# A chunked recurrence on four corners of TensorE, with merged products and one place in PSUM per chunk

## What is computed

```python
def step(state, inp):
    r_t, w_t, k_t, v_t, kk_t, a_t = inp
    sa = jnp.einsum('bhvk,bhk->bhv', state, -kk_t)
    state = (state * w_t[:, :, None, :] + sa[..., None] * (kk_t * a_t)[:, :, None, :]
             + v_t[..., None] * k_t[:, :, None, :])
    return state, jnp.einsum('bhvk,bhk->bhv', state, r_t)
...
mu = jnp.mean(y, -1, keepdims=True)
var = jnp.mean(jnp.square(y - mu), -1, keepdims=True)
y = ((y - mu) * lax.rsqrt(var + RWKV_GN_EPS)).reshape(B, T, C)
```

## Time and profile before

| | |
|---|---|
| median of three runs | 2672.34 us (2670.58 to 2675.16) |
| the profiled execution | 2671.66 us |
| its span, first to last instruction | 2669.8 us |
| TensorE (PE) busy over the span | 97% |
| VectorE (DVE) / ScalarE (ACT) / GpSimd (POOL) busy | 66% / 39% / 3% |
| mean granted TensorE clock | 0.990 |

### The profile page before, as it was taken

How to read it: one execution, slowest core, us unless ns; L and a number is a source line. 1 busy time by engine, 2 the same in 40 slices (tenths; PEclk the granted TensorE clock), 3 DMA queues, 4 the chain that set the end, 5 groups by cost and what they waited for, 6 DMA issues and landing times. The chain is left out here.

```text
span 2669.8 us, 46706 instructions
## 1 busy us (share of the span) xinstructions
PE 2600.5 (97%) x19152; PEld 2151.7 (81%) x19152; DVE 1765.2 (66%) x2819; ACT 1041.2 (39%) x1839; POOL 88.0 (3%) x121
## 2 busy tenths in 40 slices
PE   8999999999999999899999998999999999999998
PEld 7788888888777788888888887777778788888887
DVE  6877667678344564577777775853446867667676
ACT  4332223445433534344444444542343332223443
POOL 0000000000000000111111110000000000000000
PEclk9999999999999999899999999999999999999999
DMA  4332335454423388521111110630022332335454
GB/s 143 111 105 76 118 114 180 151 196 155 99 95 102 104 265 219 138 50 36 34 38 38 30 42 6 248 135 1 32 102 80 110 116 70 113 114 192 139 190 145
DMA packets 268722, 295.65 MB, mean 111 GB/s; under 512 B 64898, under 2 KB 199296, under 8 KB 268544
## 3 DMA queue, kind: packets, MB, share of 16 engines
q1 hardware_dynamic: 265808, 290.47, 34.2%
q10 hardware_dynamic: 2736, 2.65, 0.4%
HBM read 206.47 MB, written 81.36 MB: 108 GB/s over the span
## 5 line engine op out<-in xcount | busy, mean ns | idle before, releaser
L1141 PE MATMUL f_ps<-hi,f_wh 128*128 128x512 f32 x672 | 263.1, 391 | 4.1 <-DVE f_wl L847 4.1
L1143 PE MATMUL f_ps<-hi,f_wl 128*128 128x512 f32 x672 | 262.9, 391 | 0.0
L2543 PE MATMUL f_ps<-hi,f_ahead_h 128*128 128x512 f32 x392 | 164.0, 418 | 0.8 <-PEq L72 0.8
L2544 PE MATMUL f_ps<-one_lo,f_ahead_h 128*128 128x512 f32 x392 | 153.6, 392 | 0.0
L2545 PE MATMUL f_ps<-hi,f_ahead_l 128*128 128x512 f32 x392 | 153.6, 392 | 0.0
L1141 PE MATMUL f_ps<-f_t3h,f_t2h 128*128 128x512 f32 x392 | 152.5, 389 | 0.0
L1142 PE MATMUL f_ps<-f_t3l,f_t2h 128*128 128x512 f32 x392 | 152.5, 389 | 0.0
L1143 PE MATMUL f_ps<-f_t3h,f_t2l 128*128 128x512 f32 x392 | 152.5, 389 | 0.0
L1141 PEld LDWEIGHTS f_ps<-hi,f_wh 128*128 128x128 f32 x672 | 127.0, 189 | 31.2 <-DVE f_wl L847 4.9
L1143 PEld LDWEIGHTS f_ps<-hi,f_wl 128*128 128x128 f32 x672 | 126.7, 189 | 26.4
L1142 PE MATMUL f_ps<-one_lo,f_wh 128*128 128x512 f32 x352 | 137.6, 391 | 0.0
(11 more groups left out here) (584 smaller groups left out, 6830.4 us busy)
## 6 DMA issues: line engine op xcount, KB each, us to landing
act<-one_y SPq DMA_DIRECT2D x30, 512.0 KB, 3.5
f_work<-act SPq DMA_DIRECT2D x30, 512.0 KB, 3.6
act<-y SPq DMA_DIRECT2D x30, 512.0 KB, 3.6
arena<-act SPq DMA_DIRECT2D x30, 512.0 KB, 3.7
one_y<-in_w_in SPq DMA_DIRECT2D x25, 512.0 KB, 4.4
early<-in_ffn_w_gate SPq DMA_DIRECT2D x11, 1024.0 KB, 6.2
early<-in_ffn_w_up SPq DMA_DIRECT2D x11, 1024.0 KB, 8.7
f_raw<-in_ffn_w_gate SPq DMA_DIRECT2D x10, 1024.0 KB, 6.2
```

The source lines that it names most:

```text
L1141: nc.tensor.matmul(out, wh, xh, start=start, stop=False)
L1143: return nc.tensor.matmul(out, wl, xh, start=False, stop=stop)
L2543: nc.tensor.matmul(dense_ps[:, b, cols], w_hi[:, b, k, :], hi[:, k, cols], start=(k == 0), stop=False)
L2544: nc.tensor.matmul(dense_ps[:, b, cols], w_hi[:, b, k, :], lo[:, k, cols], start=False, stop=False)
```

## The change

**Crossed pairs.** For pairs 2 and 3 the results of most products go to the other half of the partitions: operand rows 0 to 63, result partitions 64 to 127, and the reverse. The matmuls of a group are issued in the order of pairs 0, 2, 1, 3, so that four in a row use the four different corners of the array. Two products, `tf` and `gr`, stay straight (`STRAIGHT`). The operands of pairs 2 and 3 are loaded into the rows that this needs, which alternates with the chunk (`crossed`): some loads become three (`load_pairs`), a second copy of two operands for these pairs is loaded (`load_across`, into an unused part of `hi`), and the end decays are exchanged between the halves once at the start of the stage (two DMAs and a copy on GpSimd).

**Merged products.** `gram_l` is part of `gram_b`; `turn_b` and `turn_k` are `turn_bk`; `turn_a` and `x` are `ax`; each level's `y` is `yt`, which also turns the inverse so far with the identity; then only `t` follows. `tt` and VectorE's `start` are gone; a product `tf` on the last level gives the turned factor for `wu`. There are 20 products per chunk where there were 27.

**One place in PSUM.** All products of a chunk are written to the same place, two pairs in each of the two banks, so each product waits until the last result has been taken out. Results of 16 matmuls are taken out in one wide copy.

**Mean.** `mean` multiplies with a centering matrix in two halves of 128 columns; ScalarE copies the centered values out and squares them from PSUM; VectorE's subtraction is gone.

The planner's assumed times are changed with it (`ON_PE`, `OUT_OF`), and so the order.

```diff
-PRODUCTS = ["gram_b", "gram_k", "gram_l", "turn_a", "turn_b", "turn_k", "x",
-            *[f"{w}{lv}" for lv in range(LEVELS) for w in (("y", "t", "tt") if lv + 1 < LEVELS else ("y", "tt"))],
-            "wu", "gr", "s", "out", "mean", "var"]
+PRODUCTS = ["gram_b", "gram_k", "turn_bk", "ax", *[f"{w}{lv}" for lv in range(LEVELS) for w in ("yt", "t") if (w, lv) != ("t", LEVELS - 1)],
+            "tf", "wu", "gr", "s", "out", "mean", "var"]
+STRAIGHT = {"tf", "gr"}
...
+def load_pairs(sp, dst, src, exchange, sem):
+    for r in range(2) if exchange else ():
+        sp.dma_start(dst[rows_of(r)], src[rows_of(1 - r)]).then_inc(sem, 16)
+    if not exchange:
+        sp.dma_start(dst, src).then_inc(sem, 16)
+
+def load_op(sp, c, which, ops, ops_dram, ops_in):
...
+    if crossed(c) == (which in (0, 3)):
+        load_pairs(sp, dst[:, 0:2], src[:, 0:2], False, ops_in[j])
+        load_pairs(sp, dst[:, 2:4], src[:, 2:4], True, ops_in[j])
+    else:
+        load_pairs(sp, dst, src, False, ops_in[j])
+
+def load_across(sp, c, ARx, ops_dram, ops_in):
+    for w, which in enumerate((0, 3)):
+        src = ops_dram[which].rearrange("(q p) t -> p q t", p=P)[:, 2:4, c * CH:(c + 1) * CH]
+        load_pairs(sp, ARx[c % 2][:, :, w, :], src, not crossed(c), ops_in[c % 2])
...
+            for r in range(2):
+                sp.dma_start(decay_x[rows(r)], end_decay[rows(1 - r), 2:4, :]).then_inc(decay_in, 16)
...
-                def group(k, lhsT, rhs, width=CH):
-                    for p in range(PAIRS):
-                        for h in range(2):
...
-                            mm = nc.tensor.matmul(at(k, p, h, width), lhsT[rows(h), p], moving, start=True, stop=True)
+                def at(p, r, block, width=CH):
+                    return ps[j][rows(r), p // 2, (p % 2 * 4 + block) * CH:(p % 2 * 4 + block) * CH + width]
+                corners = [(p, r, 1 - r if p >= 2 and name not in STRAIGHT else r) for p in (0, 2, 1, 3) for r in range(2)]
+                def group(*parts):
+                    for block, lhsT_of, rhs_of, width in parts:
+                        for p, r, to in corners:
+                            mm = nc.tensor.matmul(at(p, to, block, width), lhsT_of(p)[rows(r)], rhs_of(p)[rows(r)], start=True, stop=True)
...
+                def sum_of(*terms):
+                    for n in range(2):
+                        for x_, (lhsT_of, rhs_of) in enumerate(terms):
+                            for p, r, to in corners[4 * n:4 * n + 4]:
+                                mm = nc.tensor.matmul(at(p, to, 0), lhsT_of(p)[rows(r)], rhs_of(p)[rows(r)], start=(x_ == 0),
+                                                      stop=(x_ == len(terms) - 1))
...
+                    group((0, lambda p: B[j][:, p], unit, CH), (1, lambda p: K[j][:, p], unit, CH))
+                elif name == "ax":
...
+                    group((0, lambda p: AR[j][:, p, 0, :], unit, CH), (1, lambda p: GK[j][:, p, 0, :], lambda p: V[j][:, p], CH))
...
+                    group((0, lambda p: LTm[j][:, lv, p], lambda p: T0[j][:, p], CH), (1, lambda p: T0[j][:, p], unit, CH))
+                elif name == "tf":
+                    act(f"yt{LEVELS - 1}")
+                    group((0, lambda p: YT[j][:, p, 0, :], lambda p: YT[j][:, p, 1, :], CH))
+                elif name[0] == "t":
+                    act(f"yt{name[1:]}")
+                    group((0, lambda p: YT[j][:, p, 1, :], lambda p: YT[j][:, p, 0, :], CH))
...
+                    for n in range(2):
+                        mm = nc.tensor.matmul(features(j)[:, n * P:(n + 1) * P], center[:, 1 if n and not crossed(c) else 0, :],
+                                              yb[j][:, 2 * n:2 * n + 2].rearrange("p q c -> p (q c)"), start=True, stop=True)
...
-                    nc.vector.tensor_tensor(TT0[j][:], GB[j][:, :, 0, :], over_pairs(m_one[:, 1]), ALU.mult).then_inc(by_dve[j], 1)
-                    nc.vector.tensor_tensor(TT0[j][:], TT0[j][:], over_pairs(eye[:]), ALU.add).then_inc(by_dve[j], 1)
...
-                    for which in (("queries", 0), ("keys", 0), ("keys", 1), ("queries", 1), ("queries", 2)):
+                    for which in (("across", 0), ("queries", 0), ("keys", 0), ("keys", 1), ("queries", 1), ("across", 1), ("queries", 2)):
```

More of the change, by code:

```diff
@@ L1472, in joint_plan @@
[L1472 to L1483, removed]
+                      "yt0": [out_of("ax"), ("masked", c)],
+                      "s": [out_of("gr"), out_of("s", c - 1)],
+                      "var": [("square", c)]}.get(name, [n and out_of(PRODUCTS[n - 1])])
@@ L1484, in joint_plan @@
+            event(("rw", c, name), "pe", ON_PE.get(name, 0.47), *before)
+            event(("out_of", c, name), "dve" if name in TO_DVE else "act", OUT_OF.get(name, 0.58), ("rw", c, name),
+                  name == "s" and c and ("rw", c - 1, "out"))
+            if name == "gram_b":
+                event(("masked", c), "pool", 4.6, out_of(name))
             if name == "mean":
@@ L1627, in attend_and_recur @@
         pn = numbered(PRODUCTS)
-        dn = numbered(["gram_b", "gram_k", "gram_l", "one_t", "start", *[x for x in PRODUCTS if x in TO_DVE and x[0] == "t"], "gr_r", "gr", "mean"])
-        an = numbered(["turn_a", "turn_b", "turn_k", "x", *[f"y{lv}" for lv in range(LEVELS)], "wu", "out", "square", "var"])
+        dn = numbered(["gram_b", "gram_l", "gram_k", *[f"t{lv}" for lv in range(LEVELS - 1)], "tf", "gr_r", "gr"])
+        an = numbered(["turn_bk", "ax", *[f"yt{lv}" for lv in range(LEVELS)], "wu", "out", "mean", "square", "var"])
         gn = numbered(["one", "start", *[f"lev{lv}" for lv in range(LEVELS)]])
@@ L1637, in over_pairs, with result, by_bank, both @@
             return tile.unsqueeze(1).broadcast_to([P, PAIRS, CH])
[L1639 to L1643, removed]
+        def result(j, at, width=CH):
+            return ps[j][:].rearrange("p b (x c) -> p b x c", x=2)[:, :, :, at * CH:at * CH + width]
+        def by_bank(tile):
+            return tile.rearrange("p (b x) c -> p b x c", b=2)
+        def both(tile):
+            return tile.rearrange("p (b x) w c -> p b x (w c)", b=2)
+        def all_pairs(mask):
+            n = mask.shape[-1]
+            return mask.unsqueeze(1).unsqueeze(1).broadcast_to([P, 2, 2, n])
+        def features(j):
+            return ps[j][:, 0, 0:PAIRS * CH]
+        def across(c, p):
+            return AR[c % 2][:, p] if p < 2 else ARx[c % 2][:, p - 2]
         def chunk(c):
@@ L1812, in recur @@
                 elif name == "gram_k":
-                    if c >= 2:
-                        dve("mean", c - 2)
-                    group(1, K[j], AR[j], 2 * CH)
-                elif name == "gram_l":
-                    dve("gram_b")
-                    group(0, AR[j][:, :, 0, :], B[j])
-                elif name == "turn_a":
+                    dve("gram_l")
+                    group((0, lambda p: K[j][:, p], lambda p: flat(across(c, p)), 2 * CH))
+                elif name == "turn_bk":
@@ L1869, in recur @@
[L1869 to L1876 removed]
+                    if c:
+                        pe.wait_ge(state, c)
+                    else:
+                        pe.wait_ge(zeroed, 1)
@@ L2990, in recurrence_tables @@
         "mean_all": np.full((P, P), 1.0 / RW, f),
+        "center": np.stack([np.eye(P, dtype=f)[m] - (same.astype(f) / f(CH))[m] for m in (n, (n + CH) % P)], 1),
         "eye": (s == t).astype(f),
```

226 lines of the change are left out of this document (98 added, 128 removed).

## The result

The changed kernel takes 2568.83 us (median of four runs, 2567.76 to 2569.63) against 2673.47 us before, measured beside it (2670.58 to 2675.16): ratio 0.961, 95% interval 0.9599 to 0.9622. The forecast was 2572 us. Later measurements of the kernel before, beside the experiments, gave medians of 2672.21 to 2672.70 us, and one of the changed kernel 2567.76 us.

A forecast was written before the change was run, and what follows sets the result against it. TensorE, busy 97% of the span, was taken as the bound: 2671.7 - 112 (products) + 10 (idle) + 2 (loads) = 2571.7, so 2572 us, chance 0.66; own range 2552 to 2590, 8-in-10 range 2548 to 2615.

The forecast's parts named there:

- What bounds the stage: In the changed stage TensorE, busy 563 of 581 us, sets the pace, so time taken from it comes off the end.
- A round of four at the price of a round of two: Four matmuls on four corners take 0.117 us, as two did: products 17.5 to 10.5 us per chunk, 112 us in all.
- The number of products and matmuls is no gain: Per chunk on TensorE: 8 more small matmuls; 7 fewer group starts give only 0.35 of the 7.0 us saved.
- four corners never run at once: Rival: row halves writing the same partitions exclude each other, so small matmuls keep the old price; 2675 us, chance 0.06.
- VectorE and ScalarE: In the stage VectorE loses 57 us, leaving 369; ScalarE's wider copies add 17 us, hidden under TensorE.
- One place in PSUM costs nothing: Each product's wait for the last take-out costs nothing in itself; other chunk and attention fill TensorE meanwhile.
- Loads: SyncE's extra DMA issues, per chunk and before the stage: mostly covered, 2 us added, bounds 0 and 13.
- the mark that I named for it: Sign that the loads were mis-sized: the stage begins later than 1086 us.
- Added idle: TensorE idle in the stage grows by 10 us, as fewer long recurrence groups cover attention's round trips; bounds 0 and 34.
- VectorE as the bound: Rival: VectorE and hand-overs take over; VectorE can't be filled above 73%, stage lasts 503 us, total 2596 us; chance 0.15.
- Only wide products gain: Rival: same-row corners' weight loads come one behind the other, so 64-column products gain nothing; 2654 us, chance 0.07.
- Slower by changing between the diagonals: Rival: 112 changes per chunk between diagonal corner pairs cost 0.10 us each, 179 us in all; 2751 us, chance 0.06.

The follow-up runs named there:

- the first experiment: Changed kernel with pairs 2 and 3 writing straight, so every small matmul uses one of two corners only: 2674.36 us, ratio 1.0009 to the kernel before.
- the experiment: Changed kernel with 112 idle VectorE passes of 128x256 into unused tiles added behind take-outs: 2587.49 us, ratio 0.9697 to the kernel before.

## Why the prediction was right, step by step

*What bounds the stage* held: PE is 96% busy in it (97% before), and 15 us of added matmuls cost 11.5.

*A round of four at the price of a round of two*, the step that carries the sum, was right as far as can be read: 8 records in 0.117 us. The difference between two and four corners, costed at 112 us, is 105.5 us in the first experiment. The prices hold to the hundredth where a product of the same shape stands behind: 0.52 for `yt`, 0.28 for `t`, 0.74 for `s` against 0.75. A part of the miss is in the change to another shape, which the sum left out: there `yt` takes 0.58, `t` 0.34 and `out` 0.82.

*The number of products and matmuls is no gain*: right, since on two corners everything else gave nothing together. The case "four corners never run at once" was priced at 2675 us, and the kernel in which they don't measured 2674.

*VectorE and ScalarE*: 369 us predicted, 369.6 measured; ScalarE 17 us more predicted, 12 found (268.3 instead of 256.2).

*One place in PSUM costs nothing*: borne out by the waits. Those of PE on take-outs of the recurrence are 3.7 us for `gram_k` and under 1 us each for the others.

*Loads* (+2 us): the size is about right, the place was wrong, and so was the mark that I named for it. I looked at whether the stage would begin later; it began at 1081.5, no later than before. What came late was the first product in it, at 1093.97 instead of 1083.08. The idle time of PE in the first 34.5 us grew from 5.6 to 16.1 us, by 10.5. The loads' share is small: V and the decays put the keys 2.6 us later, and both queues reordered gave back 1.4 to 2.9 us of the stage. The larger share, some 5 to 8 us, is the order, which puts the Gram products behind the first score. That is worked out and not run by itself: 8 is what the 2.6 us leave of the 10.5, and 5 is what the order with the old prices saved of idle at the start with all loads unchanged. The sum had no term for this. The granted clock is lower there too, 0.65 over those 34.5 us against 0.80 in the kernel before over as long a stretch; what that costs by itself no run separates.

*Added idle* (+10 us) was too large, with the sign wrong: outside the start PE idles 4.7 us instead of 12.2. The fear that fewer long groups would uncover attention's round trips did not come true under this order. The order is what holds it off: with other prices for the planner 20.6 us of idle came back outside the start. I had named the order as changed and had given it no price.

So three terms were off: 105 instead of 112 gained on the products, some 10 instead of 2 lost at the start, and 7 gained instead of 10 lost in idle. With signs: -105 + 10.5 - 7.5 = -102, against -112 + 2 + 10 = -100; the profiled executions differ by 102.6. That the total came within 3 us of the forecast is partly luck, since the errors cancel. Every term lay inside its bounds but the idle, whose lower bound of 0 left out that it could fall; only the low end of the range had room for that.

*The rivals.* VectorE as the bound fell, by its 83% in the experiment. "Only wide products gain" fell with the `yt` group at 0.52 us and with four weight loads in 25 ns. The floor of about 25 ns from one matmul's start to the next, which the Trainium skill's page "TensorE: Matmul & The Clock Gate" gives in the section "Wait — 56ns, not 53.3ns?", does not hold between corners: four start within 25 ns, and over whole groups it is 14.6 ns from one start to the next. Slower by changing between the diagonals fell too: the steps of `s`, each of which goes to both diagonals, show no gap.

## What to carry to other kernels

Small matmuls of 64 by 64 should be laid out so that any four in a row of the queue use the four corners; four then cost what two do, even at 64 columns. Here that was worth 105 us. Merging products and sparing VectorE passes were worth nothing while two corners set the pace; with four corners VectorE's time begins to count, 10 to 27 us for 46.6. Where operands or sums force an order, keep the matmuls for the other corners close: with four on one diagonal ahead of them in a group, and twelve in `s` and `out`, the kernel lost 18 us, and with eight ahead in a group 48. After such a change look at the first microseconds of the stage and at the planner's order: here new loads ahead of the first operand needed took back some 1.5 to 4 us, and prices that were still the old ones 17.

## What was unexpected of the hardware

TensorE does not start matmuls strictly in the order of issue: those for a free corner overtake others. The runs show it past two matmuls that had not started, and not past four. I had expected a group laid out on one diagonal to cost the full price. And two row halves that write the same partitions in different banks of PSUM do so at the same time, with no loss that can be read: 0.117 us for four matmuls as for two.
